# Up projection: one 512-column matmul for both parts of hT, and the cross products copied and added

## The chip, the cores and the metric

The kernel runs on one core of a Trainium2 chip. The metric is the device time of one execution in microseconds (us). Five engines work side by side, each through its own queue in order: TensorE (PE: matmuls, with the weight loads shown as PEld), VectorE (DVE), ScalarE (ACT), GpSimd (POOL), and SyncE (SP), which here only issues transfers. They wait for one another on semaphores. TensorE writes into PSUM (8 banks of 512 float32 columns on 128 partitions); ScalarE and VectorE read it. SBUF is the memory that all engines work in.

## The reference

Four residual layers on x of 256 tokens by 1024. Each layer has a token mixer (forgetting attention, chunked attention, sliding window attention), then the gated MLP that this change is about, then a gated input embedding:

```python
def conv_ffn(h, w_up, conv_w, conv_b, w_down):
    u = h @ w_up                       # (256, 1024) @ (1024, 5632)
    u = causal depthwise conv of width 3 over the tokens (u, conv_w) + conv_b
    gate, up = u[..., :D_FF], u[..., D_FF:]      # D_FF = 2816
    return (jax.nn.silu(gate) * up) @ w_down
...
x = x + conv_ffn(rms_norm(x, ffn_norm[i]), w_up[i], conv_w[i], conv_b[i], w_down[i])
```

All in float32.

## The kernel before

**Split operands.** Every float32 operand of a matmul is held as two parts of a narrower format: a rounded part (`_hi`) and the rest (`_lo`). A product is three matmuls into the same bank, hi x hi, hi x lo and lo x hi: `three()` (L1294 to L1298). For weights, ScalarE makes w_hi (`split_hi`, L441), and VectorE subtracts it from the raw weights to make w_lo (`split_lo`, L744). A unit of weights is 128 x 2048, and is split in two halves of 1024 columns. `w_hi` and `w_lo` are rings of 4 units: while unit u is handled, unit u + 4 is split into the slot that unit u leaves. `w_raw` is a ring of 4 halves that SyncE fills (L417).

**The up projection** has 22 units in each layer (FC = 22), one for each 128 columns of gate and of up. `hT` is the normalised input, transposed: 8 chunks (KC) of 128 features on the partitions, 256 tokens (SEQ) along the columns. In unit k:
- TensorE (`up_unit`, L1556): for each side (gate, up) and each of 8 chunks the three matmuls of 256 columns, with the weights as the stationary operand, 48 matmuls in all. Gate goes to columns 0 to 255 and up to 256 to 511 of one bank, `up_bank` (L274), which goes round four banks. Before it starts it waits for the unit's w_lo and for `conv_done` of unit k - 4, which has used the same bank.
- ScalarE (L707): waits for the unit's matmuls; gate_c and up_c (L713, L715) are the last conv tap and the bias, out of PSUM; then both halves of w_hi for unit u + 4 (L441); Silu (L719) once the conv is done; gT_hi (L721) once the product is done.
- VectorE (L1097): the four remaining conv taps (L1108), each `tap * PSUM + gate_c` (or up_c); then both halves of w_lo for unit u + 4 (L744).
- GpSimd (L1279): the product gate_c * up_c (L1282) after Silu, and gT_lo (L1284) after gT_hi.

`over_units` (L139) makes a loop over four units at a time out of these bodies on each engine. The order on each engine is the order of the text; nothing is reordered.

**The down projection** follows: 11 units of 24 matmuls of 512 columns (`rows_unit`, L1310) with gT as the stationary operand, into the other four banks. Its first 9 units appear as one piece in the chain. ScalarE and VectorE split weights beside it.

## Time and profile before

| | |
|---|---|
| device time, median of 3 runs | 1369.4 us (1368.85 to 1369.75) |
| device time of the profiled execution | 1371.7 us |
| its span in the profile | 1369.9 us |
| TensorE busy | 1317.6 us, 96% |
| VectorE busy | 971.1 us, 71% |
| ScalarE busy | 828.6 us, 60% |
| GpSimd busy | 417.6 us, 30% |
| granted TensorE clock, mean | 0.99 |

The profile is one execution, taken by the hardware profiler. Its page has the busy time of each engine, the span in slices, and the chain of work that ended last: followed back from the last instruction, at each step to what released it. Behind it stands the trace, which can be asked for the timeline of one engine, for groups of instructions, and for the busy time in a stretch. In a timeline a row is start, duration, engine, line, operation, output and inputs, a count where like instructions are merged, and in brackets the idle time ahead of it with what ended it. A clock of 1.00 is the full 2.4 GHz. Durations of neighbouring instructions of one engine overlap a little, so costs in a sequence are read from start to start.

### The profile page before, as it was taken

The page shows a single profiled execution, that of the slowest core. Times are in us where ns is not written, and L with a number is a line of the kernel's source. Part 1 is how long each engine was busy: PE and PEld are TensorE (multiplying, and loading weights), DVE is VectorE, ACT ScalarE, POOL GpSimd, SP SyncE. Part 2 cuts the span into 40 slices and gives each one's busy share as a digit, 9 for nine tenths or more (in the row PEclk, how much of TensorE's full clock was granted, in tenths as well). Part 3 has the DMA queues.
Part 4 walks back from the last instruction along what each step waited for, and adds up shares of the span by engine and source line. Part 5 has one row for each costly group of instructions (what it writes and reads, how often), then busy time and mean ns, then how long its engine had stood idle before and what let it go on. Part 6 is the DMA issues. An engine that isn't in the chain of part 4 may idle for free.

```text
span 1369.9 us, 24686 instructions
## 1 busy us (share of the span) xinstructions
PE 1317.6 (96%) x8340; PEld 1174.1 (86%) x8340; DVE 971.1 (71%) x1531; ACT 828.6 (60%) x1469; POOL 417.6 (30%) x523
## 2 busy tenths in 40 slices
PE   5999999999999999999996799999999999999998
PEld 4878999988788899998875689998887788999887
DVE  4677877755777777774588687776476787777635
ACT  4676666644568666663465666665365786666533
POOL 3541233310265123330037313332014520333200
PEclk9999999999999999999998899999999999999999
DMA  8533655555664456656543155556556335555651
GB/s 289 165 129 102 206 184 182 181 194 177 198 226 136 151 177 184 184 184 201 174 156 108 47 170 184 184 184 194 175 177 200 123 110 184 182 181 179 195 184 62
DMA packets 64311, 232.89 MB, mean 170 GB/s; under 512 B 7312, under 2 KB 7440, under 8 KB 64240
## 3 DMA queue, kind: packets, MB, share of 16 engines
q1 hardware_dynamic: 61344, 221.87, 50.1%
q0 software_dynamic: 2896, 10.08, 2.6%
q8 instruction: 44, 0.72, 0.2%
q14 instruction: 27, 0.22, 0.1%
HBM read 230.87 MB, written 1.05 MB: 169 GB/s over the span
## 4 chain that ended last, share of the span: by engine, by line
PE 80%; DVE 9%; ACT 4%; POOL 3%; issue 2%; DMA 2%; SPq 0%; POOLq 0%; DVEq 0%; ACTq 0%
PE bank L1320 23%; PE bank L1296 17%; PE bank L1297 16%; PE bank L1298 16%; DVE w_lo L744 4%; PE bank L1335 3%; DMA w_raw<-weights 2%; PE bank L1465 2%; PE bank L1488 1%; DVE tok L787 1%; ACT w_hi L441 1%; ACT tok L464 1%; ACT hT_hi L472 1%; PE bank L1385 1%; POOL hrstd L1141 1%
## 5 line engine op out<-in xcount | busy, mean ns | idle before, releaser
L744 DVE TENSOR_TENSOR w_lo<-w_raw,w_hi 128x1024 fp32r<-128x1024 f32 x418 | 556.3, 1367 | 124.3 <-ACT w_hi L441 123.3
L441 ACT ACTIVATE w_hi<-w_raw 128x1024 fp32r<-128x1024 f32 x418 | 422.2, 1056 | 150.4 <-PE bank L1320 117.4
L1296 PE MATMUL bank<-hT_hi,w_hi 128*128 128x256 f32 x1408 | 398.7, 283 | 2.1 <-DVE hT_lo L795 2.1
L1298 PE MATMUL bank<-hT_hi,w_lo 128*128 128x256 f32 x1408 | 398.4, 283 | 0.0
L1297 PE MATMUL bank<-hT_lo,w_hi 128*128 128x256 f32 x1408 | 398.4, 283 | 0.0
L1296 PEld LDWEIGHTS bank<-hT_hi,w_hi 128*128 128x128 f32 x1408 | 270.3, 192 | 3.7 <-issue 3.7
L1298 PEld LDWEIGHTS bank<-hT_hi,w_lo 128*128 128x128 f32 x1408 | 270.3, 192 | 0.0
L1297 PEld LDWEIGHTS bank<-hT_lo,w_hi 128*128 128x128 f32 x1408 | 270.3, 192 | 0.0
L1282 POOL TENSOR_TENSOR gate_c<-gate_c,up_c 128x256 f32<-128x256 f32 x88 | 105.1, 1194 | 288.6 <-ACT gate_c L719 288.6
L1108 DVE SCALAR_TENSOR_TENSOR gate_c<-bank,conv_sb,gate_c 128x255 f32<-128x255 f32 (+1 forms) x176 | 84.1, 478 | 116.6 <-ACT up_c L715 116.6
L1296 PE MATMUL bank<-w_hi,hT_hi 128*128 128x512 f32 (+1 forms) x336 | 135.2, 402 | 7.9 <-DVE w_lo L744 4.2
L1297 PE MATMUL bank<-w_lo,hT_hi 128*128 128x512 f32 (+1 forms) x336 | 130.8, 389 | 0.0
L1298 PE MATMUL bank<-w_hi,hT_lo 128*128 128x512 f32 (+1 forms) x336 | 130.6, 389 | 0.0
L1146 POOL TENSOR_TENSOR ssq<-ssq 128x1 f32<-128x1 f32 x24 | 7.5, 315 | 378.5 <-ACT tok L464 378.5
L721 ACT ACTIVATE gT_hi<-gate_c 128x256 f32 (+1 forms) x88 | 36.8, 419 | 122.2 <-POOL gate_c L1282 122.2
L1284 POOL TENSOR_TENSOR gT_lo<-gate_c,gT_hi 128x256 f32 (+1 forms) x88 | 84.4, 959 | 63.5 <-ACT gT_hi L721 63.5
L1320 PE MATMUL bank<-w_hi,gT_hi 128*128 128x512 f32 x320 | 98.6, 389 | 0.0
L1320 PE MATMUL bank<-w_lo,gT_hi 128*128 128x512 f32 x320 | 98.6, 389 | 0.0
L1320 PE MATMUL bank<-w_hi,gT_lo 128*128 128x512 f32 x320 | 98.5, 389 | 0.0
L713 ACT ACTIVATE gate_c<-bank,conv_sb 128x256 f32<-128x256 f32 x88 | 49.7, 565 | 67.1 <-PE bank L1298 67.1
L1296 PEld LDWEIGHTS bank<-w_hi,hT_hi 128*128 128x128 f32 x336 | 63.9, 190 | 24.7 <-DVE w_lo L744 5.9
L1108 DVE SCALAR_TENSOR_TENSOR up_c<-bank,conv_sb,up_c 128x255 f32<-128x255 f32 (+1 forms) x176 | 83.3, 474 | 0.1
(159 smaller groups left out, 2096.8 us busy)
## 6 DMA issues: line engine op xcount, KB each, us to landing
w_raw<-weights SPq DMA_DIRECT2D x418, 512.0 KB, 4.1
gain<-gains POOLq DMA_DIRECT2D x11, 512.0 KB, 4.9
rel<-rel_in POOLq DMA_DIRECT2D x8, 256.0 KB, 3.6
x<-x_in SPq DMA_DIRECT2D x2, 512.0 KB, 6.3
p_raw<-p_in POOLq DMA_DIRECT2D x4, 256.0 KB, 5.2
out<-x SPq DMA_DIRECT2D x4, 256.0 KB, 2.6
gain<-gains SPq DMA_DIRECT2D x1, 512.0 KB, 6.8
consts<-consts_in POOLq DMA_DIRECT2D x1, 392.0 KB, 3.6
```

The lines of the kernel that those rows point to most:

```text
L441: nc.scalar.activation(w_hi[:, slot, q * HALF:(q + 1) * HALF], w_raw[:, raw, :], ACT.Copy).then_inc(hi_ready, 1)
L713: nc.scalar.activation(gate_c[:, b, :], up_bank(L, slot)[:, 0:SEQ], ACT.Identity, bias=c[:, 3:4], scale=c[:, 2:3]).then_inc(conv_first, 1)
L721: nc.scalar.activation(gT_hi[:, k, :], gate_c[:, b, :], ACT.Copy).then_inc(gT_hi_ready, 1)
L744: nc.vector.tensor_tensor(w_lo[:, slot, cols], w_raw[:, half(q)[0], :], w_hi[:, slot, cols].bitcast(F32), ALU.subtract).then_inc(lo_ready, 1)
L1108: ins = nc.vector.scalar_tensor_tensor(buf[:, b, lag:SEQ], up_bank(L, slot)[:, side * SEQ:side * SEQ + SEQ - lag], c[:, 4 * side + tap:4 * ...
L1282: nc.gpsimd.tensor_tensor(gate_c[:, b, :], gate_c[:, b, :], up_c[:, b, :], ALU.mult).then_inc(prod_done, 1)
L1284: nc.gpsimd.tensor_tensor(gT_lo[:, k, :], gate_c[:, b, :], gT_hi[:, k, :].bitcast(F32), ALU.subtract).then_inc(gT_ready, 1)
L1296: nc.tensor.matmul(out_ap, l_hi, r_hi, start=start, stop=False, skip_group_check=True)
L1297: nc.tensor.matmul(out_ap, l_hi, r_lo, start=False, stop=False, skip_group_check=True)
L1298: return nc.tensor.matmul(out_ap, l_lo, r_hi, start=False, stop=stop, skip_group_check=True)
L1320: last = nc.tensor.matmul(banks[2 * t + b][:, :], l[:, c, ts], w[:, slot, col:col + 512], start=(c == 0 and l is left_hi and w is w_hi), s ...
L1335: last = nc.tensor.matmul(banks[2 * t + b][:, :], l[:, c, ts], w[:, slot, col:col + 512], start=False, stop=(j == 1 and l is left_lo), ski ...
```

## The change

hT_hi and hT_lo become the two halves of one tile, so that for each chunk a single matmul of 512 columns with w_hi as the stationary operand gives w_hi x hT_hi in columns 0 to 255 and w_hi x hT_lo in columns 256 to 511 of a bank. The third product, w_lo x hT_hi, is a matmul of 256 columns into columns 0 to 255. Gate and up now have a bank each, so a unit takes two of the four banks, and TensorE waits for the sum of unit k - 2. ScalarE copies the cross products of both sides to SBUF (`cross_c`); VectorE adds them to the main ones (`both_c`); the conv reads `both_c` in SBUF in place of PSUM. The first half of w_hi and of w_lo moves ahead of the conv's work on its engine, the second half stays behind it.

```diff
--- before.py
+++ after.py
@@ -171,8 +171,8 @@
         w_lo = sb("w_lo", [P, RING, UNIT], F32R)
         x = sb("x", [P, TT, D])
         tok = sb("tok", [P, TT, D])
-        hT_hi = sb("hT_hi", [P, KC, SEQ], F32R)
-        hT_lo = sb("hT_lo", [P, KC, SEQ], F32R)
+        hT = sb("hT", [P, KC, 2, SEQ], F32R)
+        hT_hi, hT_lo = hT[:, :, 0, :], hT[:, :, 1, :]
         gain = sb("gain", [P, D])
         ident = sb("ident", [P, P])
         consts = sb("consts", [P, C_END])
@@ -203,6 +203,8 @@
             gT_lo = sb("gT_lo", [P, FC, SEQ], F32R, ffn)
             gate_c = sb("gate_c", [P, 2, SEQ], F32, ffn)
             up_c = sb("up_c", [P, 2, SEQ], F32, ffn)
+            cross_c = sb("cross_c", [P, 2, SEQ], F32, ffn)
+            both_c = sb("both_c", [P, 2, SEQ], F32, ffn)
             pp = sb("pp", [P, TT, D], F32, ffn)
         with ExitStack() as early:
             p_raw = sb("p_raw", [P, 2, SEQ], F32, early)
@@ -239,7 +241,8 @@
             return sc_tok[:, slot, :] if slot < 4 else sc_gain[:, slot - 4, :]
 
 
-        bank = [ctx.enter_context(nc.psum_tensor(f"bank{i}", [P, 512], F32)) for i in range(8)]
+        psum = ctx.enter_context(nc.psum_tensor("bank", [P, 8, 512], F32))
+        bank = [psum[:, i, :] for i in range(8)]
         acc, aux = bank[:4], bank[4:]
 
         maskF = consts[:, C_MASKF:C_MASKF + SEQ]
@@ -271,8 +274,10 @@
         def pt_bank(h):
             return acc[2 + h % 2]
 
-        def up_bank(L, slot):
-            return aux[(slot - FIRST_UP[L]) % RING]
+        def up_banks(L, slot):
+
+            b = 4 + 2 * ((slot - FIRST_UP[L]) % 2)
+            return psum[:, b:b + 2, :]
 
         o_banks = [acc[0], acc[1], aux[0], aux[1]]
         ple_banks = [aux[2], aux[3], acc[2], acc[3]]
@@ -346,6 +351,8 @@
         o_ready = sem("o_ready")
         esink_ready = sem("esink_ready")
         gainT_ready = sem("gainT_ready")
+        cross_out = sem("cross_out")
+        up_sum = sem("up_sum")
         conv_first = sem("conv_first")
         conv_tap = sem("conv_tap")
         conv_done = sem("conv_done")
@@ -450,8 +457,11 @@
                 u = first + j // 2 + RING
                 split_hi(u, u % RING, half_of(u), halves=(j % 2,))
 
+            def later(half):
+                return lambda q: (half(q)[0], half(q)[1] + 2 * RING // RAW)
+
             def split_looped(u, slot, half, k):
-                split_hi(u + RING, slot, lambda q: (half(q)[0], half(q)[1] + 2 * RING // RAW))
+                split_hi(u + RING, slot, later(half))
 
             def square(n, t):
 
@@ -707,14 +717,19 @@
                 def up_unit(u, slot, half, k):
                     b = slot % 2
                     act.wait_ge(unit_used, u + 1)
+                    if not isinstance(k, int) or FC * L + k >= 1:
+                        act.wait_ge(up_sum, k + FC * L)
+                    nc.scalar.activation(cross_c[:], up_banks(L, slot)[:, :, SEQ:2 * SEQ], ACT.Copy).then_inc(cross_out, 1)
+                    split_hi(u + RING, slot, later(half), halves=(0,))
+                    act.wait_ge(up_sum, k + (FC * L + 1))
                     c = conv_sb[:, L, k, :]
                     if not isinstance(k, int) or FC * L + k >= 2:
                         act.wait_ge(gT_ready, k + (FC * L - 1))
-                    nc.scalar.activation(gate_c[:, b, :], up_bank(L, slot)[:, 0:SEQ], ACT.Identity,
+                    nc.scalar.activation(gate_c[:, b, :], both_c[:, 0, :], ACT.Identity,
                                          bias=c[:, 3:4], scale=c[:, 2:3]).then_inc(conv_first, 1)
-                    nc.scalar.activation(up_c[:, b, :], up_bank(L, slot)[:, SEQ:2 * SEQ], ACT.Identity,
+                    nc.scalar.activation(up_c[:, b, :], both_c[:, 1, :], ACT.Identity,
                                          bias=c[:, 7:8], scale=c[:, 6:7]).then_inc(conv_first, 1)
-                    split_looped(u, slot, half, k)
+                    split_hi(u + RING, slot, later(half), halves=(1,))
                     act.wait_ge(conv_done, k + (FC * L + 1))
                     nc.scalar.activation(gate_c[:, b, :], gate_c[:, b, :], ACT.Silu).then_inc(silu_done, 1)
                     act.wait_ge(prod_done, k + (FC * L + 1))
@@ -1097,7 +1112,9 @@
                 def up_unit(u, slot, half, k):
                     b = slot % 2
                     c = conv_sb[:, L, k, :]
-
+                    dve.wait_ge(cross_out, k + (FC * L + 1))
+                    nc.vector.tensor_tensor(both_c[:], up_banks(L, slot)[:, :, 0:SEQ], cross_c[:], ALU.add).then_inc(up_sum, 1)
+                    split_lo(u + RING, slot, half, halves=(0,))
                     dve.wait_ge(conv_first, k * 2 + (2 * FC * L + 2))
                     for tap in (1, 0):
                         lag = 2 - tap
@@ -1106,12 +1123,12 @@
 
                                 dve.wait_ge(conv_tap, k * 2 + (2 * FC * L + side + 1))
                             ins = nc.vector.scalar_tensor_tensor(
-                                buf[:, b, lag:SEQ], up_bank(L, slot)[:, side * SEQ:side * SEQ + SEQ - lag],
+                                buf[:, b, lag:SEQ], both_c[:, side, 0:SEQ - lag],
                                 c[:, 4 * side + tap:4 * side + tap + 1], buf[:, b, lag:SEQ], ALU.mult, ALU.add)
                             if tap == 1:
                                 ins.then_inc(conv_tap, 1)
                     ins.then_inc(conv_done, 1)
-                    split_looped(u, slot, half, k)
+                    split_lo(u + RING, slot, half, halves=(1,))
 
                 over_units(dve, FIRST_UP[L], FC, up_unit)
                 over_units(dve, FIRST_DOWN[L], DOWN_UNITS - DOWN_TAIL, split_looped)
@@ -1556,15 +1573,18 @@
                 def up_unit(u, slot, half, k):
 
                     wait_unit(u)
-                    if not isinstance(k, int) or FC * L + k >= RING:
-                        pe.wait_ge(conv_done, k + (FC * L + 1 - RING))
+                    if not isinstance(k, int) or FC * L + k >= 2:
+                        pe.wait_ge(up_sum, k + (FC * L - 1))
                     for side in range(2):
                         for c in range(KC):
                             if side == 0 and c in (0, KC // 2):
                                 pe.wait_ge(hT_ready, 4 * (n0 + 1) + (3 if c == 0 else 4))
                             col = slice(c * 256 + side * P, c * 256 + (side + 1) * P)
-                            last = three(up_bank(L, slot)[:, side * SEQ:(side + 1) * SEQ], w_hi[:, slot, col], w_lo[:, slot, col],
-                                         hT_hi[:, c, :], hT_lo[:, c, :], c == 0, c == KC - 1)
+                            into = up_banks(L, slot)[:, side, :]
+                            nc.tensor.matmul(into, w_hi[:, slot, col], hT[:, c, :, :], start=c == 0, stop=c == KC - 1,
+                                             skip_group_check=True)
+                            last = nc.tensor.matmul(into[:, 0:SEQ], w_lo[:, slot, col], hT_hi[:, c, :], start=False,
+                                                    stop=c == KC - 1, skip_group_check=True)
                     last.then_inc(unit_used, 1)
 
                 over_units(pe, FIRST_UP[L], FC, up_unit, peel=L == 0)
```

## Rows read from the trace of the kernel before

**Rows 1.** Page, parts 1 and 2: busy time; TensorE's clock in 40 slices.

```profile
PE 1317.6 (96%) x8340; PEld 1174.1 (86%) x8340; DVE 971.1 (71%) x1531; ACT 828.6 (60%) x1469; POOL 417.6 (30%) x523
...
PEclk9999999999999999999998899999999999999999
```

**Rows 2.** Page, part 4: the chain of work that ended last, by line.

```profile
PE bank L1320 23%; PE bank L1296 17%; PE bank L1297 16%; PE bank L1298 16%; DVE w_lo L744 4%; PE bank L1335 3%; DMA w_raw<-weights 2%; PE bank L1465 2%; PE bank L1488 1%; DVE tok L787 1%; ACT w_hi L441 1%; ACT tok L464 1%; ACT hT_hi L472 1%; PE bank L1385 1%; POOL hrstd L1141 1%
```

**Rows 3.** Timeline of TensorE, first up matmul of layers 0 and 3.

```profile
149.67 0.36 PE L1296 MATMUL bank<-hT_hi,w_hi 128*128 128x256 f32 x1 [0.53 <-DVE hT_lo L795]
...
1154.64 0.36 PE L1296 MATMUL bank<-hT_hi,w_hi 128*128 128x256 f32 x1 [0.53 <-DVE hT_lo L795]
```

**Rows 4.** Chain in order of time, down units (start us, us, what).

```profile
276.62 48.99 PE bank L1320 x216
...
1281.59 48.99 PE bank L1320 x216
```

**Rows 5.** Stretch, length, busy of PE, PEld, DVE, ACT, POOL; clock, DMA.

```profile
149.67:276.62 126.95, 126.95 (x1057) 126.95 (x1058) 98.82 (x132) 80.79 (x129) 45.15 (x42) 1.00 0.59 184
```

**Rows 6.** Timeline of ScalarE: first up unit, then one in mid-stage.

```profile
155.69 0.57 ACT L713 ACTIVATE gate_c<-bank,conv_sb 128x256 f32<-128x256 f32 x1 [2.91 <-PE bank L1298]
...
202.05 0.56 ACT L713 ACTIVATE gate_c<-bank,conv_sb 128x256 f32<-128x256 f32 x1 [0.73 <-PE bank L1298]
202.51 0.56 ACT L715 ACTIVATE up_c<-bank,conv_sb 128x256 f32<-128x256 f32 x1
202.96 2.00 ACT L441 ACTIVATE w_hi<-w_raw 128x1024 fp32r<-128x1024 f32 x2
204.92 0.42 ACT L719 ACTIVATE gate_c<-gate_c 128x256 f32<-128x256 f32 x1
206.75 0.42 ACT L721 ACTIVATE gT_hi<-gate_c 128x256 f32 x1 [1.41 <-POOL gate_c L1282]
207.74 0.57 ACT L713 ACTIVATE gate_c<-bank,conv_sb 128x256 f32<-128x256 f32 x1 [0.58 <-PE bank L1298]
```

**Rows 7.** Timeline of VectorE: the same unit in mid-stage.

```profile
203.23 0.48 DVE L1108 SCALAR_TENSOR_TENSOR gate_c<-bank,conv_sb,gate_c 128x255 f32<-128x255 f32 x1 [1.37 <-ACT up_c L715]
...
204.80 2.90 DVE L744 TENSOR_TENSOR w_lo<-w_raw,w_hi 128x1024 fp32r<-128x1024 f32 x2
```

**Rows 8.** Timeline of GpSimd: the same unit in mid-stage.

```profile
205.41 1.20 POOL L1282 TENSOR_TENSOR gate_c<-gate_c,up_c 128x256 f32<-128x256 f32 x1 [2.95 <-ACT gate_c L719]
207.36 0.94 POOL L1284 TENSOR_TENSOR gT_lo<-gate_c,gT_hi 128x256 f32 x1 [0.74 <-ACT gT_hi L721]
```

**Rows 9.** Timeline of ScalarE: copies from PSUM; w_hi in the down stage.

```profile
145.63 1.09 ACT L472 ACTIVATE hT_hi<-bank 128x512 fp32r<-128x512 f32 x2
146.59 1.08 ACT L441 ACTIVATE w_hi<-w_raw 128x1024 fp32r<-128x1024 f32 x1
...
282.12 1.06 ACT L441 ACTIVATE w_hi<-w_raw 128x1024 fp32r<-128x1024 f32 x1 [0.57 <-PE bank L1320]
```

**Rows 10.** Groups by form (xcount, busy us, mean ns, idle before): an add.

```profile
L764 DVE TENSOR_TENSOR x<-x,bank 128x512 f32<-128x512 f32 x32 | 21.2, 684 | 16.3 <-PE bank L1335 16.1
```

**Rows 11.** Timeline of VectorE: w_lo elsewhere; two inputs in SBUF.

```profile
150.04 1.21 DVE L744 TENSOR_TENSOR w_lo<-w_raw,w_hi 128x1024 fp32r<-128x1024 f32 x1
...
283.21 2.36 DVE L744 TENSOR_TENSOR w_lo<-w_raw,w_hi 128x1024 fp32r<-128x1024 f32 x2 [1.04 <-ACT w_hi L441]
...
341.90 1.42 DVE L787 SCALAR_TENSOR_TENSOR tok<-x,rstd,gain 128x512 f32<-128x512 f32 x2 [2.04 <-POOL rstd L1141]
343.23 2.35 DVE L744 TENSOR_TENSOR w_lo<-w_raw,w_hi 128x1024 fp32r<-128x1024 f32 x2
```

**Rows 12.** The same view, two stretches in which TensorE has gaps.

```profile
768.00:772.00 4.00, 3.35 (x26) 2.65 (x27) 3.45 (x16) 3.22 (x13) 1.07 (x3) 1.00 0.02 4
756.00:760.00 4.00, 0.21 (x2) 0.25 (x4) 2.47 (x7) 1.92 (x7) 2.54 (x4) 0.50 0.00 0
```

**Rows 13.** Page, part 6: transfers of weights, KB, us to landing.

```profile
w_raw<-weights SPq DMA_DIRECT2D x418, 512.0 KB, 4.1
```


## The prediction, made before the changed kernel was run

> **What bounds the kernel now.** I read the shares of busy time first: TensorE is busy 96% of the span, VectorE 71%, ScalarE 60%, and the clock granted to TensorE is near full in every slice [rows 1]. The chain of work that ended last then says whose time it is: 72% of the span is on the three matmul groups of `three()` and `rows_unit` (L1320, L1296 to L1298) [rows 2]. So a TensorE instruction that goes away is worth something, as long as TensorE stays the engine that others wait for.
>
> The edit touches one stage, the up projection, which runs four times. In layer 0 its first matmul starts at 149.67 [rows 3], the down projection takes over at 276.62 [rows 4], and in these 126.95 us TensorE has no idle time at all at a clock of 1.00 [rows 5]. The other three layers repeat this (the last one: 1154.64 to 1281.59 [rows 3, 4]). With 22 units of 48 matmuls each, a unit costs 126.95 / 22 = 5.77 us and a 256-column matmul 5.77 / 48 = 0.1202 us. The busy durations of single matmuls overlap and don't sum. The four stages are 508 of 1370 us.
>
> What the other engines do inside one unit decides the question, since TensorE is idle for none of it and they have slack. ScalarE works through a fixed order [rows 6]: gate_c at 202.05, up_c at 202.51, the two halves of w_hi from 202.96, Silu at 204.92, gT_hi at 206.75, and the next gate_c at 207.74 after 0.58 us of waiting for TensorE. That 0.58 us is all the slack there is in this round: were the unit's matmuls faster, ScalarE could come round every 5.77 - 0.58 = 5.19 us or so. VectorE has its four conv taps from 203.23 to 204.80 and then two halves of w_lo [rows 7], GpSimd a product and a difference [rows 8]. The gap of 1.41 us in ScalarE ahead of gT_hi is that product. Nothing of unit u+1 is started on ScalarE before gT_hi of unit u: the four engines take turns, and one round of them is a serial chain.
>
> **TensorE's part of the change.** Removed: the 16 matmuls of 256 columns with hT_lo; the 16 with hT_hi and w_hi grow to 512 columns and give both products; the 16 with w_lo stay. The columns streamed are the same. A 512-column matmul costs 48.99 / 216 = 0.2268 us in the down stage [rows 4]. A unit becomes 16 x 0.2268 + 16 x 0.1202 = 5.55 us, 0.22 us less than 5.77. If TensorE stayed the bound this would be 88 x 0.22 = 19.4 us off the kernel. That the matmul does not reach 0.2268 when hT is the moving operand is possible, but by what follows it has over 1 us per unit to hide in.
>
> The Trainium skill (TensorE: Matmul & The Clock Gate, section Back-to-back issue gap) gives N / 2.4 + 2.5 ns per warm matmul. By it a unit would go from 48 x 109.2 = 5.24 us to 16 x 215.8 + 16 x 109.2 = 5.20 us (an estimate from that page), so almost nothing is saved by halving the number of instructions. This trace shows 0.1202 and 0.2268 us in place of 0.109 and 0.216, and the measurement decides.
>
> **The round of the other engines.** Let 0 be the start of the new copy of the cross products on ScalarE. The copy reads 512 columns of PSUM; a like copy (L472) has its successor start 0.48 us after it (two in the 0.96 us from 145.63 to 146.59 [rows 9]) and lasts 0.60. Then:
> - w_hi, first half: starts 0.48, lasts 1.06 [rows 9], ends 1.54. It is now ahead of gate_c and up_c.
> - VectorE meanwhile starts the new add at about 0.64, when the copy has ended. Its price is that of a 512-column add with one input in PSUM, 0.68 us [rows 10], so up_sum stands at 1.32. This lies beside w_hi and costs the round nothing; ScalarE reaches gate_c at about 1.46 anyway.
> - w_lo, first half, now stands in VectorE's queue ahead of the taps. It starts at 1.54 + 0.04 (283.18 to 283.21 in the down stage, rounded up) and takes 1.14 us: a pair without GpSimd beside it takes 2.36 and a single one 1.21, so the two start about 1.14 apart [rows 11]. It ends at 2.72.
> - gate_c and up_c: from 1.46, with 0.46 between them and 0.56 for the second [rows 6], end 2.48; the first tap started 0.16 us after that in the trace [rows 6, 7], which is 2.64. They now read SBUF, which the trace doesn't show with these operands. The SBUF-only Silu at 0.42 us is below them, and this edge gives nothing away either way: w_lo ends later, at 2.72.
> - Four taps: 204.80 - 203.23 = 1.57 us [rows 7], to T = 4.29. They too now read SBUF in place of PSUM. Lower bound: the slope of w_lo, 1.14 us for 1024 columns, gives 0.28 us for 255, or 1.14 in all. Upper bound: the whole duration of 0.47 to 0.48 with no overlap, 1.9. Nearest row: the same operation with both inputs in SBUF at 512 columns, two of them in 1.33 us from start to start (341.90 to 343.23 [rows 11]), 0.665 each; less 257 columns of that slope that is 0.38. I keep 1.57.
> - From T to gT_hi: Silu, the product on GpSimd, the handoffs. In the trace that is 206.75 - 204.80 = 1.95 us with a half of w_lo starting at T [rows 6, 7, 8], and after the change a half of w_lo starts at T again. gT_hi starts at 6.24.
> - gT_hi 0.42 us [rows 6], then the next copy. The next instruction could start 0.1 us sooner, as up_c does after gate_c; in a loop I don't count on it. The round is **6.66 us**. The second halves of w_hi (from about 2.4 to 3.4 on ScalarE) and of w_lo (4.29 to 5.4 on VectorE) hide in it. VectorE's work in a round is 0.68 + 1.57 + 2 x 1.14, GpSimd's two operations stay under 2.2 us: neither is a bound alone. It is the chain.
>
> Against the old order this is 1.5 us more between the first look at a unit's PSUM and T (4.29 against 204.80 - 202.05 = 2.75), and 0.9 us more than the 5.77 us of TensorE. So the bound passes from TensorE to this chain.
>
> One rule of the skill bears on the 1.95 us. What the rows show: the pair of w_lo that starts at 204.80 lasts 2.90 us where it lasts 2.36 in the down stage [rows 7, 11], and the product that is issued in it shows 1.20 us [rows 8]; 0.54 us between the two pairs. The Trainium skill (SBUF — State Buffer, section Who interferes with whom) says that a VectorE instruction with two SBUF inputs and a GpSimd instruction that reads SBUF lock each other out, and that the later one blocks until the other has finished. By that rule, the trace agrees: the product waits for the first half of w_lo to end at T + 1.14, runs some 0.6 to 0.7 us, and the second half waits for it. The new taps come under the same rule, with both inputs in SBUF, but in the new order gT_lo of the unit before runs at about 0.1 to 0.8, under the add, which has one SBUF input, and the product comes after the taps. The sum is the same by the rule and by the row.
>
> **The stage.** `up_sum` lets TensorE run two units ahead. Unit 0 ends 5.55 us after the stage's start, and ScalarE's first instruction on it follows 0.25 us later (155.69 - 149.67 = 6.02 against 5.77 [rows 3, 6]): 5.80. The copy of unit 19 is at 5.80 + 19 x 6.66 = 132.34. Unit 21 may start once the sum of unit 19 is done, 1.32 later, and takes 5.55: the stage is 139.2 us, 12.3 more than 126.95. TensorE idles about 1.1 us in each round. What comes after the stage: ScalarE is two units behind and needs some 13 us to finish them, in which TensorE has down units 0 to 2 at 5.44 us each, whose weights are split in the rounds of units 18 to 20. So the backlog is hidden, and nothing is given back. If that cover failed it would be a few us per layer. The new operands move no DMA: weights for unit u+4 are asked for two rounds before they are split and land in 4.1 us [rows 13].
>
> **Sum.** 4 x 12.3 = 49 us on the profiled execution's 1371.7: 1421. The median of the runs shown is 2.3 us below the profiled one, so I forecast **1418.7 us**. Each 0.1 us of the round is 19 x 4 x 0.1 = 7.6 us.
>
> **The rivals.**
> - *TensorE keeps the bound*, and the 0.22 us per unit come through: 1369.4 - 19.4 = 1350 us, faster. Its place is the handoff from `up_sum` to the second-next unit, and because of the two units of lead it decides at a round of (126.95 - 5.80 - 1.32 - 5.55) / 19 = 6.01 us, not at 5.77. For it speaks that VectorE is at only 71%; against it that the chain would have to be 0.65 us shorter than the rows add up to, more than the taps' lower bound (0.43) gives alone. 5%; another 2% for a round near 6.0 that gives no change.
> - *The product is not held up by w_lo.* If it ran at once, the round would be 0.54 shorter, 6.12, and the time 1378. The rows with 2.90 us speak against it. 4%.
> - *Every handoff in the loop costs more*: gate_c and up_c not overlapped from SBUF, taps at their upper bound (+0.34), a further 0.1 in the copy. The round is 7.1, the time 1452. 15%.
> - *TensorE's clock falls.* The gaps of 1.1 us could cost the granted clock. At 0.50 a unit takes 11.1 us, 22 of them 244 us, and the kernel some 1840 us. In the trace the clock is at half (1.2 GHz) in a stretch where TensorE was busy 0.21 of 4 us, and at full (2.4 GHz) where it was busy 3.35 of 4 us [rows 12]; with 5.55 of 6.66 busy, the same 84%, this stage is like the latter. 3%.
>
> **How the numbers follow.** The forecast case, a round of 6.3 to 7.0, has the remaining 71%. The range: the taps' lower bound puts the round at 6.23 (1386), the upper one at 7.0 (1445); I take 1388 to 1453, which leaves out the clock case, the case of the product that is not held up, the two with a round near 6.0 or below, and under half of the slow one. Faster by over 0.2% 0.05, within 0.2% (about what a measurement of this kernel can tell from no change) 0.02, slower 0.93.
>
> **What would show it.** In the profile of the changed kernel: TensorE idle about 1.1 us ahead of each up unit, released by the add on VectorE; its clock still 1.00; ScalarE's copy starting every 6.66 us straight behind gT_hi with no wait for TensorE; taps starting when the first half of w_lo ends; up stages of 139 us and down stages as before. I am wrong if TensorE is busy throughout the stage, if the taps wait for up_c and not for w_lo, or if rounds differ from 6.66 by over 0.4 us.

## The result and the profile after

The changed kernel takes 1426.9 us (median of 4 runs, 1426.0 to 1427.7) against 1369.6: a ratio of 1.041, 95% interval 1.038 to 1.044, 57 us slower. The forecast was 1418.7, slower, with a range of 1388 to 1453.

The page of after, parts 1 and 2: busy time of each engine, TensorE and its clock in slices.

```profile
PE 1325.2 (93%) x6932; PEld 1100.0 (77%) x6932; DVE 990.7 (70%) x1619; ACT 882.9 (62%) x1557; POOL 398.9 (28%) x523
...
PE   5999998899999998889995899889999999988998
...
PEclk9999999999999999999998899999999999999999
```

TensorE went from 96% busy to 93%, with 1408 fewer matmuls, and its clock is as near to full as in [rows 1]. The digits show 8 in the later part of each up stage, where the same row of the kernel before has 9:

```profile
PE   5999999999999999999996799999999999999998
```

Busy time by stretch, in the columns of [rows 5]: the up stages of layers 0 and 1.

```profile
149.53:289.13 139.60, 127.20 (x705) 107.43 (x706) 99.12 (x147) 89.89 (x145) 38.28 (x40) 1.00 0.50 163
497.75:638.58 140.83, 128.29 (x705) 107.82 (x706) 99.46 (x146) 90.33 (x145) 38.16 (x40) 1.00 0.49 162
```

The first takes 139.60 us where [rows 5] has 126.95, and TensorE stands still for 12.4 of them, at a clock of 1.00. The chain in order of time has the down units:

```profile
289.13 48.97 PE bank L1337 x216
...
638.58 49.00 PE bank L1337 x216
...
979.11 48.98 PE bank L1337 x216
...
1336.75 49.00 PE bank L1337 x216
```

They last as long as in [rows 4]. With the first up matmuls at 149.53, 497.75, 838.23 and 1195.28, the four up stages last 139.60, 140.83, 140.88 and 141.47 us, 562.8 in all against 4 x 126.95 = 507.8. These 55.0 us are the whole difference between the two profiled spans (1425.1 and 1369.9, 55.2 us). Nothing was lost or won elsewhere.

One round in mid-stage of the changed kernel. Timeline of ScalarE:

```profile
200.90 0.42 ACT L736 ACTIVATE gT_hi<-gate_c 128x256 f32 x1 [1.41 <-POOL gate_c L1299]
201.23 0.58 ACT L722 ACTIVATE cross_c<-bank 128x512 f32<-128x512 f32 x1
201.70 1.05 ACT L448 ACTIVATE w_hi<-w_raw 128x1024 fp32r<-128x1024 f32 x1
202.77 0.60 ACT L728 ACTIVATE gate_c<-both_c,conv_sb 128x256 f32<-128x256 f32 x1
203.28 0.59 ACT L730 ACTIVATE up_c<-both_c,conv_sb 128x256 f32<-128x256 f32 x1
203.77 1.04 ACT L448 ACTIVATE w_hi<-w_raw 128x1024 fp32r<-128x1024 f32 x1
205.73 0.42 ACT L734 ACTIVATE gate_c<-gate_c 128x256 f32<-128x256 f32 x1 [0.91 <-DVE up_c L1125]
207.55 0.42 ACT L736 ACTIVATE gT_hi<-gate_c 128x256 f32 x1 [1.41 <-POOL gate_c L1299]
208.06 0.60 ACT L722 ACTIVATE cross_c<-bank 128x512 f32<-128x512 f32 x1
```

Timeline of VectorE:

```profile
201.84 0.69 DVE L1116 TENSOR_TENSOR both_c<-bank,cross_c 128x512 f32<-128x512 f32 x1 [1.66 <-ACT cross_c L722]
202.78 1.23 DVE L759 TENSOR_TENSOR w_lo<-w_raw,w_hi 128x1024 fp32r<-128x1024 f32 x1 [0.25 <-ACT w_hi L448]
204.03 0.48 DVE L1125 SCALAR_TENSOR_TENSOR gate_c<-both_c,conv_sb,gate_c 128x255 f32<-128x255 f32 x1
...
205.21 0.48 DVE L1125 SCALAR_TENSOR_TENSOR up_c<-both_c,conv_sb,up_c 128x254 f32<-128x254 f32 x1
205.61 1.22 DVE L759 TENSOR_TENSOR w_lo<-w_raw,w_hi 128x1024 fp32r<-128x1024 f32 x1
208.69 0.69 DVE L1116 TENSOR_TENSOR both_c<-bank,cross_c 128x512 f32<-128x512 f32 x1 [1.86 <-ACT cross_c L722]
```

Timeline of GpSimd:

```profile
206.22 1.20 POOL L1299 TENSOR_TENSOR gate_c<-gate_c,up_c 128x256 f32<-128x256 f32 x1 [3.98 <-ACT gate_c L734]
208.16 0.73 POOL L1301 TENSOR_TENSOR gT_lo<-gate_c,gT_hi 128x256 f32 x1 [0.74 <-ACT gT_hi L736]
```

Timeline of TensorE, two of the up matmuls that it stood still ahead of:

```profile
209.44 0.50 PE L1584 MATMUL bank<-hT,w_hi 128*128 128x512 f32 x1 [1.01 <-DVE both_c L1116]
...
216.17 0.50 PE L1584 MATMUL bank<-hT,w_hi 128*128 128x512 f32 x1 [0.92 <-DVE both_c L1116]
```

This is the serial round of the prediction. ScalarE's copy starts right behind gT_hi with no wait for TensorE in front of it (in [rows 6] gate_c waited 0.58 us for TensorE). TensorE runs through the first seven units of layer 0 without a gap, on its lead of two units; then it waits 0.7 to 1.0 us ahead of each unit (the prediction said about 1.1), and where the profile names a releaser it is VectorE's add. The product shows 1.20 us, because it stands behind the second half of w_lo (e2 below tests this).

What lets the taps start is not what the prediction said. Up_c ends at 203.28 + 0.59 = 203.87, and the first tap starts 0.16 us later at 204.03, the same 0.16 us as in [rows 6, 7]; it stands 1.25 us behind the start of w_lo, though VectorE needs 1.14 only. So the taps wait for up_c. In the first four units of layer 0, whose bodies are written out on ScalarE, it is w_lo: there the tap follows its start by 1.15 us, with up_c done 0.2 us earlier. Timeline of ScalarE in such a unit:

```profile
163.74 0.59 ACT L730 ACTIVATE up_c<-both_c,conv_sb 128x256 f32<-128x256 f32 x1
```

Timeline of VectorE:

```profile
163.38 1.23 DVE L759 TENSOR_TENSOR w_lo<-w_raw,w_hi 128x1024 fp32r<-128x1024 f32 x1 [0.26 <-ACT w_hi L448]
164.53 0.48 DVE L1125 SCALAR_TENSOR_TENSOR gate_c<-both_c,conv_sb,gate_c 128x255 f32<-128x255 f32 x1
```

By these distances the taps wait for up_c in the 76 units that ScalarE runs in its loop, and for w_lo in the 12 that are written out there (the first four of layer 0 and the last two of each layer).

### The profile page after: what moved, and what is told of

Its sections match the earlier page's. It is cut to its first block, busy times and chain, and to the rows that moved or that the text cites. A ratio compares the mean times of both kernels' runs of the same rounds, so it can differ in the third digit from the quotient of the medians.

```text
span 1425.1 us, 22301 instructions
## 1 busy us (share of the span) xinstructions
PE 1325.2 (93%) x6932; PEld 1100.0 (77%) x6932; DVE 990.7 (70%) x1619; ACT 882.9 (62%) x1557; POOL 398.9 (28%) x523
## 4 chain that ended last, share of the span: by engine, by line
PE 51%; DVE 14%; ACT 14%; issue 10%; POOL 8%; DMA 2%; ACTq 1%; DVEq 1%; SPq 0%; POOLq 0%
PE bank L1337 22%; PE bank L1584 8%; POOL gate_c L1299 5%; ACT w_hi L448 5%; DVE w_lo L759 5%; PE bank L1313 4%; PE bank L1586 4%; PE bank L1315 3%; PE bank L1314 3%; PE bank L1352 3%; DVE up_c L1125 3%; ACT up_c L730 2%; DMA w_raw<-weights 2%; ACT gate_c L734 2%; PE bank L1482 2%
## 5 line engine op out<-in xcount | busy, mean ns | idle before, releaser
L1584 PE MATMUL bank<-hT,w_hi 128*128 128x512 f32 x1408 | 504.3, 401 | 52.8 <-DVE both_c L1116 41.4
L1586 PE MATMUL bank<-hT,w_lo 128*128 128x256 f32 x1408 | 394.2, 280 | 0.0
L1584 PEld LDWEIGHTS bank<-hT,w_hi 128*128 128x128 f32 x1408 | 264.2, 188 | 135.4 <-DVE both_c L1116 58.4
L1586 PEld LDWEIGHTS bank<-hT,w_lo 128*128 128x128 f32 x1408 | 265.7, 189 | 0.0
L1313 PE MATMUL bank<-w_hi,hT 128*128 128x512 f32 (+1 forms) x336 | 135.8, 404 | 7.2 <-DVE w_lo L759 3.9
L1315 PE MATMUL bank<-w_hi,hT 128*128 128x512 f32 (+1 forms) x336 | 131.7, 392 | 0.0
L1314 PE MATMUL bank<-w_lo,hT 128*128 128x512 f32 (+1 forms) x336 | 131.5, 391 | 0.0
L1337 PE MATMUL bank<-w_hi,hT 128*128 128x512 f32 x384 | 108.1, 393 | 0.0
L1125 DVE SCALAR_TENSOR_TENSOR gate_c<-both_c,conv_sb,gate_c 128x255 f32<-128x255 f32 (+1 forms) x176 | 84.5, 480 | 3.8 <-ACT up_c L730 1.1
L1125 DVE SCALAR_TENSOR_TENSOR up_c<-both_c,conv_sb,up_c 128x255 f32<-128x255 f32 (+1 forms) x176 | 84.1, 478 | 0.0
L1313 PEld LDWEIGHTS bank<-w_hi,hT 128*128 128x128 f32 x336 | 64.4, 192 | 23.6 <-DVE w_lo L759 5.7
L1337 PEld LDWEIGHTS bank<-w_hi,hT 128*128 128x128 f32 x384 | 71.2, 188 | 14.8
```

Of the source, the lines that this page charges most:

```text
L1125: ins = nc.vector.scalar_tensor_tensor(buf[:, b, lag:SEQ], both_c[:, side, 0:SEQ - lag], c[:, 4 * side + tap:4 * side + tap + 1], buf[:, b ...
L1313: nc.tensor.matmul(out_ap, l_hi, r_hi, start=start, stop=False, skip_group_check=True)
L1314: nc.tensor.matmul(out_ap, l_hi, r_lo, start=False, stop=False, skip_group_check=True)
L1315: return nc.tensor.matmul(out_ap, l_lo, r_hi, start=False, stop=stop, skip_group_check=True)
L1337: last = nc.tensor.matmul(banks[2 * t + b][:, :], l[:, c, ts], w[:, slot, col:col + 512], start=(c == 0 and l is left_hi and w is w_hi), s ...
L1584: nc.tensor.matmul(into, w_hi[:, slot, col], hT[:, c, :, :], start=c == 0, stop=c == KC - 1, skip_group_check=True)
```

## The experiments

All times are medians. The kernel before ran beside each group of experiments, at 1371 to 1372 us; in the comparison above it was 1369.6, so differences of 1 or 2 us between experiments and the changed kernel say nothing.

**Is it the round, or the banks? (e1)** The changed kernel gives each unit two of four banks, so TensorE may lead by two units in place of four. That is a second reason why it might stand still. The first experiment leaves the banks alone and takes ScalarE out of its wait for the product:

```diff
@@ ScalarE, up_unit @@
                     split_hi(u + RING, slot, later(half), halves=(0,))
+                    if not isinstance(k, int) or k >= 1:
+                        act.wait_ge(prod_done, k + FC * L)
+                        nc.scalar.activation(gT_hi[:, k - 1, :], gate_c[:, 1 - b, :], ACT.Copy).then_inc(gT_hi_ready, 1)
                     act.wait_ge(up_sum, k + (FC * L + 1))
...
-                    act.wait_ge(prod_done, k + (FC * L + 1))
-                    nc.scalar.activation(gT_hi[:, k, :], gate_c[:, b, :], ACT.Copy).then_inc(gT_hi_ready, 1)
```

The last unit's gT_hi follows the loop, whose first four units are written out.

> The changed kernel with one step moved: ScalarE rounds gT_hi of unit k-1 in the round of unit k, behind the first half of w_hi, so that it no longer stands still for the product. If the serial round ScalarE, VectorE, GpSimd is what costs 57 us, the round falls from 6.72 us to at most 5.7 (gate_c at 1.87 after the copy, the first tap at about 3.35 because gT_lo may hold VectorE up, conv done at 4.9, next copy at 5.45), TensorE is the bound again at 5.55 us a unit, and the time is 1370 - 19 = 1350 us (1347 to 1357). The rival, that two banks a unit (a lead of two units in place of four) or the wait for the sum itself hold TensorE back, keeps the time at 1415 to 1427, since neither is touched.

Measured: 1355.2 us, ratio 0.988 (0.986 to 0.990) to the kernel before. One moved instruction takes 72 us off the changed kernel, and the result beats both. Timeline of ScalarE:

```profile
201.07 0.60 ACT L722 ACTIVATE cross_c<-bank 128x512 f32<-128x512 f32 x1 [0.22 <-PE bank L1589]
...
202.51 0.41 ACT L726 ACTIVATE gT_hi<-gate_c 128x256 f32 x1
...
205.97 0.42 ACT L737 ACTIVATE gate_c<-gate_c 128x256 f32<-128x256 f32 x1 [1.11 <-DVE up_c L1128]
206.62 0.60 ACT L722 ACTIVATE cross_c<-bank 128x512 f32<-128x512 f32 x1 [0.23 <-PE bank L1589]
```

The copy waits for TensorE again (0.22 us), gT_hi no longer waits for anything, and the round is 5.55 us, TensorE's own (5.65 in layer 2 of this execution, with TensorE busy throughout at a clock of 1.00; why its matmuls took 2% longer there is open). So neither the two banks nor the wait for the sum hold TensorE back by anything that these runs can tell: copy, add and new order are all still there, and the next experiment, without copy and add, is 2 us faster.

**The matmul alone (e5)**, without copy and add:

```diff
+        hT = sb("hT", [P, KC, 2, SEQ], F32R)
...
-            return aux[(slot - FIRST_UP[L]) % RING]
+            return aux[2 * ((slot - FIRST_UP[L]) % 2) + side]
...
+                            nc.tensor.matmul(into, w_hi[:, slot, col], hT[:, c, :, :], start=c == 0, stop=c == KC - 1, skip_group_check=True)
+                            last = nc.tensor.matmul(into[:, 0:SEQ], w_lo[:, slot, col], hT_hi[:, c, :], start=False, stop=c == KC - 1, skip_group_check=True)
```

> The kernel before with the matmul part alone: one tile for hT, the 512-column matmul, two banks a unit, TensorE waiting for the conv of unit k-2. There is no copy and no add: the conv reads the columns 0 to 255 of each bank in PSUM and leaves out the products of w_hi with hT_lo; splits stay behind the conv. If the price of the change lies in copy, add and order, TensorE stays the bound at 16 x 0.2268 + 16 x 0.1202 = 5.55 us a unit, and the time is 1369.6 - 19.4 = 1350 us (1348 to 1353). If two banks a unit are the trouble, it is above 1370.

Measured: 1353.0 us, ratio 0.988 (0.985 to 0.991), 18.9 us below the kernel before on that chip. The matmul does what the sum said; the rest of the change loses more than it gains.

**The matmul undone**, in the changed kernel (e3) and in the one with gT_hi moved (e7):

```diff
-                            nc.tensor.matmul(into, w_hi[:, slot, col], hT[:, c, :, :], start=c == 0, stop=c == KC - 1, skip_group_check=True)
+                            nc.tensor.matmul(into[:, 0:SEQ], w_hi[:, slot, col], hT_hi[:, c, :], start=c == 0, stop=False, skip_group_check=True)
+                            nc.tensor.matmul(into[:, SEQ:2 * SEQ], w_hi[:, slot, col], hT_lo[:, c, :], start=False, stop=c == KC - 1, skip_group_check=True)
```

> The changed kernel with the 512-column matmul cut into two of 256 columns again (48 matmuls a unit, same results). If the round of the other engines is the bound, only the first and last unit of a stage show it: 4 x 2 x 0.22 = 1.8 us, 1428.7 us (1427 to 1431). If TensorE's own time still set the pace, it is 88 x 0.22 = 19 us more: 1446.

> The kernel with gT_hi in the next round (e1) and, on top of it, the 512-column matmul cut into two of 256. In e1 TensorE is the bound again at 5.55 us a unit. If so, the matmul's 0.22 us a unit now counts in full: 88 x 0.22 = 19 us more than e1, that is 1.4% above it and the time of the kernel before, 1370 to 1375 us. In after the same cut cost 0.8 us. If e1 is bound by something else than TensorE, the cut costs it 0 to 5 us.

Measured: 1427.7 us in the changed kernel (1426.9), so there the larger matmul buys nothing that can be told from zero. On top of e1 the same edit costs 16 us where 19 was the sum: 1371.2, ratio 1.000 (0.999 to 1.001) to the kernel before. Once TensorE is the bound, all of what e1 gains is the matmul.

**The hold-up between w_lo and the product (e2).** The prediction took 1.95 us from the end of the taps to gT_hi, with the product held up by a half of w_lo. In this experiment that half waits for the product:

```diff
                     ins.then_inc(conv_done, 1)
+                    dve.wait_ge(prod_done, k + (FC * L + 1))
                     split_lo(u + RING, slot, half, halves=(1,))
```

> The changed kernel with a wait added: VectorE starts the second half of w_lo only when GpSimd's product is done. If the product is held up for 0.54 us in each round by that half of w_lo, the round goes from 6.72 to 6.18 us and the time from 1427 to 1427 - 76 x 0.54 = 1386 us (1382 to 1392), although a wait was added and VectorE ends 0.2 us later. If the two only share and the product takes 1.2 us anyway, there is no change or a few us more: 1427 to 1435.

Measured: 1403.5 us, so an added wait made the kernel 23 us faster, and not 41. Timeline of GpSimd:

```profile
204.00 0.73 POOL L1300 TENSOR_TENSOR gate_c<-gate_c,up_c 128x256 f32<-128x256 f32 x1 [3.70 <-ACT gate_c L734]
```

Timeline of VectorE:

```profile
204.86 1.23 DVE L759 TENSOR_TENSOR w_lo<-w_raw,w_hi 128x1024 fp32r<-128x1024 f32 x1 [1.39 <-POOL gate_c L1300]
206.01 0.69 DVE L1116 TENSOR_TENSOR both_c<-bank,cross_c 128x512 f32<-128x512 f32 x1
...
211.35 1.23 DVE L759 TENSOR_TENSOR w_lo<-w_raw,w_hi 128x1024 fp32r<-128x1024 f32 x1 [1.39 <-POOL gate_c L1300]
212.49 0.68 DVE L1116 TENSOR_TENSOR both_c<-bank,cross_c 128x512 f32<-128x512 f32 x1
```

The product takes 0.73 us when nothing holds it up, against 1.20: the hold-up is real and costs 0.47 us. Some 0.2 us of it is lost again, since the delayed half of w_lo now stands ahead of the next add (204.86 plus 1.15 is 206.01; the second add starts at 212.49, and the copy before it had ended at 212.26), and gate_c waits for that add. Rounds in mid-loop are 6.38 us, 0.27 below those of the changed kernel (6.65).

**The loop (e6).** ScalarE's copies in the changed kernel start at these distances: 6.45 us in the four units of layer 0 that are written out on ScalarE (VectorE and GpSimd have them in their loops), and 6.65, 6.65, 6.83, 6.75 in turn in the loop. So the bodies were written out on ScalarE, VectorE and GpSimd; the same edit stands on all three, here ScalarE's:

```diff
-                over_units(act, FIRST_UP[L], FC, up_unit, peel=L == 0)
+                over_units(act, FIRST_UP[L], FC, up_unit, unroll=True)
```

> The changed kernel with the up projection's bodies on ScalarE, VectorE and GpSimd written out for all 22 units in place of a loop over four (TensorE's loop stays). In after, the rounds of the written-out units take 6.45 us and those of the loop 6.65, 6.65, 6.83, 6.75, mean 6.72. If the handoffs in the loop are what my sum left out, the round is 6.45 everywhere: 16 rounds of layer 0 and 19 of each other layer save 0.27 us, 73 x 0.27 = 20 us, 1427 - 20 = 1407 us (1403 to 1411). If the loop costs nothing and the first rounds are short for another reason, the time stays within 1424 to 1430.

Measured: 1405.2 us, ratio 1.026 (1.024 to 1.029). Timeline of ScalarE, in units that are in the loop in after:

```profile
205.00 0.42 ACT L740 ACTIVATE gT_hi<-gate_c 128x256 fp32r<-128x256 f32 x1 [1.32 <-POOL gate_c L1303]
205.32 0.58 ACT L726 ACTIVATE cross_c<-bank 128x512 f32<-128x512 f32 x1
...
211.45 0.42 ACT L740 ACTIVATE gT_hi<-gate_c 128x256 fp32r<-128x256 f32 x1 [1.31 <-POOL gate_c L1303]
211.77 0.58 ACT L726 ACTIVATE cross_c<-bank 128x512 f32<-128x512 f32 x1
```

Every round is 6.45 us. The gap ahead of gT_hi is 1.32 us in place of 1.41, and no copy comes 0.51 us after gT_hi's start, as the one at 208.06 does in the changed kernel. The taps start 2.70 us after the copy in place of 2.80, released by w_lo and no longer by up_c. The 0.09 and the 0.10 make nearly all of the 0.20 us between 6.45 and 6.65; the rest of the 0.27 comes at the loop's turn. Since four rounds of the changed kernel have 6.45 us with ScalarE alone written out, the 0.20 us belong to ScalarE's loop. There the trace has a sequencer instruction, FUSED_REGOPS, once for each looped unit at gT_hi (52 ns) and at up_c (74 ns), and in this experiment none. That these instructions are the cause is likely, but no run tests them by themselves.

**The order of the splits (e4).** Both halves behind the conv, as before:

```diff
-                    split_hi(u + RING, slot, later(half), halves=(0,))
...
-                    split_hi(u + RING, slot, later(half), halves=(1,))
+                    split_hi(u + RING, slot, later(half))
@@ VectorE @@
-                    split_lo(u + RING, slot, half, halves=(0,))
...
-                    split_lo(u + RING, slot, half, halves=(1,))
+                    split_lo(u + RING, slot, half)
```

> The changed kernel with the order of before for the splits: both halves of w_hi and both of w_lo behind the conv, copy and add kept. From the rows of after: sum at 1.32, gate_c at 1.37, up_c ends at 2.46, first tap 2.62, conv done 4.19 in place of 4.38; but both halves of w_lo and the product between them now stand ahead of the next add, 2.95 us. The round is 6.5 us plus 0.07 for the loop against 6.72: 76 x 0.15 = 11 us less, 1427 - 11 = 1416 us (1410 to 1422). If moving a half of the split ahead of the conv was what cost most of the 57 us, it falls to 1390 or below.

Measured: 1516.6 us, 90 above the changed kernel, where 11 below was expected. Timeline of VectorE:

```profile
206.80 0.47 DVE L1123 SCALAR_TENSOR_TENSOR up_c<-both_c,conv_sb,up_c 128x254 f32<-128x254 f32 x1
207.19 2.35 DVE L758 TENSOR_TENSOR w_lo<-w_raw,w_hi 128x1024 fp32r<-128x1024 f32 x2
```

Timeline of GpSimd:

```profile
207.80 2.34 POOL L1297 TENSOR_TENSOR gate_c<-gate_c,up_c 128x256 f32<-128x256 f32 x1 [3.98 <-ACT gate_c L733]
```

My expectation had the product run between the two halves of w_lo, as it does in [rows 7, 8], where the pair lasts 2.90 us and the product 1.20. Here the pair lasts 2.35, undisturbed, and the product 2.34: it waited for both halves. It was issued 0.61 us after the first half's start, just as in [rows 7, 8]. What differs at this place is that the four taps in front of the pair read SBUF.

TensorE's clock fell in this run: 0.965 over the execution, where the changed kernel has 0.989. TensorE mostly stands still for about 2 us ahead of a unit here. Stretches in the columns of [rows 5]:

```profile
200.00:220.00 20.00, 15.58 (x79) 12.86 (x77) 11.71 (x17) 9.57 (x16) 9.20 (x6) 0.91 0.43 144
...
240.00:260.00 20.00, 14.01 (x77) 11.49 (x77) 10.92 (x16) 10.17 (x18) 8.41 (x6) 1.00 0.47 153
```

From 205.33 to 208.52 a pair of matmuls takes 0.64 us in place of 0.35, which is the lower of the two levels, 1.2 GHz. Inside the rounds this is hidden, since ScalarE's copy still follows gT_hi by 0.33 us with no wait for TensorE; it shows in the last unit of the stage, where in three of four layers some 1.6 us more go by than in the changed kernel, some 5 us of the 90.

Two experiments on this kernel followed. In one (e8) the taps read PSUM:

```diff
-                                buf[:, b, lag:SEQ], both_c[:, side, 0:SEQ - lag],
+                                buf[:, b, lag:SEQ], up_banks(L, slot)[:, side, 0:SEQ - lag],
...
-                        pe.wait_ge(up_sum, k + (FC * L - 1))
+                        pe.wait_ge(conv_done, k + (FC * L - 1))
```

> The kernel with the splits behind the conv (e4), with the four taps reading the bank in PSUM again, as in the kernel before; they leave out the cross products, which only the ScalarE parts of gate_c and up_c then have. TensorE therefore waits for the conv of unit k-2 in place of its sum, which puts some 2.9 us on each stage, 11 us in all. In e4 the product waited for both halves of w_lo (2.33 us, round 7.83); in before and in the matmul-alone kernel it came in between the halves (1.20 us, the pair 2.90). The one difference at that place is where the taps read. If six operations in a row with both inputs in SBUF keep GpSimd out until the last, and taps from PSUM let it in after the first half, the product is back at 1.20 us and the round at 6.5 plus 0.07: 1516 - 76 x 1.26 + 11 = 1431 us (1420 to 1440). If the taps have nothing to do with it (placement of tiles, the order alone), the product stays at 2.33 and the time at 1516 + 11 = 1527 us.

and in the other (e9) a small memset comes between the halves:

```diff
+                    split_lo(u + RING, slot, half, halves=(0,))
+                    nc.vector.memset(spare[:], 0.0)
+                    split_lo(u + RING, slot, half, halves=(1,))
```

> e4 with a memset of 8 columns on VectorE between the two halves of w_lo; the taps read SBUF as in e4. If GpSimd gets its turn as soon as VectorE runs an operation that doesn't read two SBUF inputs, the product shows 1.2 us, the pair of w_lo 2.9, the round 6.6, and the time is 1516 - 76 x 1.2 = 1425 us (1415 to 1435), although an instruction was added. If what keeps GpSimd out is something else, the time stays at 1516 to 1522 us.

Measured: 1438.7 us with the taps in PSUM (its pair of w_lo lasts 2.90 us, its product 1.20), 1425.3 us with the memset. Timeline of VectorE with the memset:

```profile
200.45 2.90 DVE L759 TENSOR_TENSOR w_lo<-w_raw,w_hi 128x1024 fp32r<-128x1024 f32 x2
201.62 0.07 DVE L1131 MEMSET spare<- 128x8 f32 x1
```

Timeline of GpSimd with the memset:

```profile
201.06 1.20 POOL L1300 TENSOR_TENSOR gate_c<-gate_c,up_c 128x256 f32<-128x256 f32 x1 [3.79 <-ACT gate_c L734]
```

With either edit the pair is back at 2.90 us and the product at 1.20. An added instruction of 0.07 us takes 91 us off. So what VectorE runs around the waiting operation decides. In e8 the difference at this place is what the taps read. In e9 it can be that the memset reads nothing from SBUF, or only that another instruction stands there: a small operation with two SBUF inputs in its place was not tried. Why two halves of w_lo in a row let GpSimd in between them when the taps in front read PSUM, and not when they read SBUF, stays open.

## Why the prediction was right, and what it sized wrong

- *What bounds before, and the matmul's 0.22 us a unit*: right. The matmul alone gave 18.9 us of 19.4, and nothing in the changed kernel (0.8 us between 32 and 48 matmuls a unit).
- *The bound passes to a serial round ending in gT_hi*: right. e1 shows it, since moving that one step gave back all of the loss and 1.2% more. Three rivals fell: that TensorE keeps the bound, that its clock falls (1.00 in the up stages), and that the product is not held up. The one of dearer handoffs came true in part, at a round of 6.72 and not of 7.1.
- *What releases the taps*: wrong. The prediction had w_lo end at 2.72, after up_c's edge at 2.64, and named taps that wait for up_c as a sign of being wrong. They wait for up_c in 76 of 88 units. Gate_c starts 1.54 after the copy (forecast 1.46), up_c 0.51 behind it (0.46) and lasts 0.59 (0.56), so that the first tap starts at 2.80. VectorE is through with w_lo at 202.78 + 1.14, which is 2.69 from the copy. The two edges lie so close together that the round is only 0.1 us longer by it; that the forecast hardly suffered is owed to that.
- *The terms of the round*, read from the copy at 201.23: end of the copy to the add 0.03 (0.04); VectorE free of the first half of w_lo at 2.69 (2.72); first tap at 2.80 (2.72); last tap's successor at 4.38 (4.29); four taps 1.58 (1.57), so reading SBUF in place of PSUM changed nothing; from there to gT_hi 1.94 (1.95); gT_hi to the next copy 0.33, and 0.51 once in four (0.42). gate_c and up_c take 0.60 and 0.59 us from SBUF, more than the 0.56 from PSUM. At the loop's turn gate_c starts 1.64 after the copy (209.70).
- *The mis-sized terms.* The profiled executions differ by 55.2 us where the sum had 49. The mean round is 6.66 in layer 0 and 6.72, 6.72 and 6.75 in the others against 6.66: with 19 rounds in each layer, 3.9 us in all. The first copy comes 6.00 us after the stage's start in three layers, not 5.80: 0.6 us. From the copy of unit 19 to the down units it is 7.30 us in layer 0 (281.83 to 289.13) and 7.2 to 7.3 in the others, where I had 1.32 + 5.55 = 6.87: TensorE starts 0.11 us after the sum is done (282.44 + 0.69, 283.24), and its last unit takes 5.7 us. In four layers this is 1.5 us. These make up the 6 us. The round had no term for the turn of the loop; that it came out within 0.1 us in spite of it is luck, because the written-out rows of layer 0 and an overlap that I didn't count (0.33 for 0.42) lean the other way. e6 prices the loop as a whole at 0.27 us a round, 22 us in all. The other 2 us by which the median missed the forecast are the 2.3 that I took off because the profiled execution of before stood above its median; that of after (1426.9) stands at it.
- *The rule on two SBUF inputs*: the sum was the same by rule and row for this kernel, and e2 confirms the hold-up. My own expectation of e4 fell: the rule as the Trainium skill (SBUF — State Buffer, section Who interferes with whom) states it, that the later one blocks until the other has finished, does not tell that a waiting GpSimd operation can be passed over by the next VectorE operation. The measurement decides: 2.34 us.

## What to carry to other kernels

Before an operation is taken off a saturated engine by adding steps to others, write down one round of the others from start to start, in queue order, and see which of them stands still for another's result: their busy shares (71%, 60%) did not show it here. Where the round is the bound, look for the instruction that waits in the middle of an in-order queue and move it behind the next unit's first work; here that made 72 us, where freeing the product made 23 and writing out the loop 22, and it alone makes the larger matmul worth its 1.2%.

## What the runs showed that I had not expected

- Six VectorE operations in a row with two SBUF inputs (four taps, two halves of w_lo) kept a GpSimd operation waiting through the end of the sixth: 2.34 us for one that takes 0.73 alone. With the taps reading PSUM, or with a memset of 8 columns after the fifth operation, it waited only for the operation during which it was issued, 1.20 us in all. In this kernel that is 78 to 91 us, of which some 5 are the clock that fell in e4.
- A round of the same work is 6.45 us written out and 6.72 on average in a loop over four units, most of it by ScalarE's loop, although no engine is near its limit. Where TensorE is the bound nothing of it is seen: e1, with the same loops on VectorE and GpSimd and ScalarE's from the fifth unit on, keeps TensorE's 5.55 us.
